# Ring, split units and attention tail of a hybrid mixer with 32 experts: five expert steps into dead buffers, high parts first, earlier splits

## The chip, the cores and the metric

One core of a Trainium2 chip runs one program. The time is the device time of a launch in microseconds, the median of three runs of the kernel before. TensorE, VectorE, ScalarE, GpSimd and SyncE each work through their own list of instructions and wait for each other by semaphores; SyncE does nothing but issue DMAs here.

## What is computed

Input `x` is 1 x 256 x 1024 in fp32. The first block adds to it a hybrid mixer and a mixture of experts, the second block four mixers: attention with a forgetting gate (`fox0`), gated linear attention (`gla`), gated delta net (`gdn`), and a second attention (`fox1`). Every layer begins with an RMS norm and two kinds of dense products, an input projection and an output projection. Cut to what matters here:

```python
def first_block(x, ...):
    hn = rmsnorm(h, norm_mix)                 # SSD + short convolution
    h = h + hybrid_mixer(hn, w_in, ..., w_out)
    hn = rmsnorm(h, norm_ffn)                 # 4 groups x 8 experts, best 2 of a group
    h = h + hierarchical_moe(hn, w_router_group, w_router_expert, w_gate, w_up, w_down)
    return rmsnorm(h, final_norm)
...
    def run_block(args):                      # one expert, d = 1024, f = 512
        return (jax.nn.silu(xb @ w_gate[e]) * (xb @ w_up[e])) @ w_down[e]
...
def fox_mixer(xn, w_in, b_f, q_gain, k_gain, w_out):
    q, k, v, z, f_logit = jnp.split(xn @ w_in, ...)      # 8 heads of 128
    ... p = softmax(q k / sqrt(dh) + (cum_q - cum_k), causal); o = p v
    return (o * jax.nn.silu(z)) @ w_out
```

## The kernel before

**Weights in a ring.** All big weights pass through `ring`, four slots of 2 MB (128 x 4096 fp32). SyncE loads a slot in two halves of 1 MB (`put`, lines 411 to 416) as soon as the slot's last user has released it (`released`, 326 to 332): a block of a dense layer is released when VectorE has split its last unit (`low_ready`), a step of the experts when TensorE has multiplied with it (`ring_used`). SyncE issues in program order: `ssd` (11 blocks of the input projection, 4 of the output projection), the experts, then `fox0`, `gla`, `gdn`, `fox1`.

**Dense units.** An fp32 product is made of three products of reduced operands (`F32R`): w_h x_h, w_h x_l and w_l x_h, with `_h` the rounded value and `_l` what is left. A block of weights has four units. For each unit ScalarE writes `w_h` (`high`, line 549), VectorE subtracts to get `w_l` (`low`, 919), each into one of three buffers (`PARTS`), so unit u waits until TensorE is done with u - 3. The activations lie as `hnT_h` and `hnT_l`; they are written by the norm (`norm_copies` 584, `norm` 967 and 971) and, ahead of an output projection, pair by pair of 128-row tiles by ScalarE (`out_high`, 573) and VectorE (`out_low`, 933). TensorE waits for `low_ready` of the unit and then runs it through `products` (lines 1669 to 1671), k after k, the three products of one k behind each other: in a `channels` unit 8 k x 3 matmuls of 256 columns with the weights stationary, in a `tokens` unit, and in all output projections, 2 token tiles x 2 k x 3 matmuls of 512 columns with the activations stationary. Who calls it: `project` (input), `gate_unit` (the eight gate units of an attention, one per head), `out_projection` (eight units, two k each; the first four wait for a pair of activations each). There are 132 units of the first kind and 72 of the second.

**Experts.** Eight quads of four experts, each quad 12 steps of 2 MB: 8 up steps (gate and up alternate; line 1892), 4 down steps (1913). Every expert has 32 places, so four experts fill the 128 columns of the array side by side. Between the up steps and the down steps of a quad stand the next quad's gather (1881), tanh on ScalarE (703), two products on VectorE, transposes; after the down steps the scatter (1924) and the sum into `x_res`. The first four steps are in the ring before the router is done; the other 92 are loaded when a slot comes free. The weights of all quads are read once (`passes` is 1 unless an expert has more than 32 tokens).

**Order around the experts.** The SSD layer ends with two groups of output units (`out_projection("ssd", [0])` and `[1]`; between them squares, their sums at 1721 and the spread at 1740), then transposes (1855), the router products (1862, which count `rt_done`), ranking on VectorE, gather, quad 0.

**Attention** (`fox`, three functions of the same name on ScalarE, VectorE, TensorE). After six projection blocks TensorE waits for all 12 bank copies, does gate unit 0, half of the key norms' spread (1740), gate unit 1, the other half, the scores of heads 0 and 1, and then per head h: gate unit h + 2, values of head h - 1 (2010 to 2012), transposes of the probabilities (2001), scores of head h + 2 (1992). ScalarE makes exponentials (743), copies the turned probabilities (749) and takes the gate's tanh (753); VectorE makes logits and their maxima (1365 to 1372), normalizes (1377 to 1379), gates (1385, 1393). In the same loops ScalarE and VectorE split the coming unit's weights (`high(z0 + h + 5)`, `low(z0 + h + 5)`), and from h = 6 on an output pair each. At the end TensorE runs

```python
                values(5)
                turn(6)
                out_projection(name, steps=[0])
                values(6)
                turn(7)
                out_projection(name, steps=[1])
                values(7)
                out_projection(name, steps=range(2, 2 * UNITS))
```

Names of semaphores that the change uses: `sq_summed` (sums of squares done), `unit_done` (dense units done), `rt_done` (router products), `fox_l` (logits of a head), `hnT_high` and `hnT_own` (high halves of the norm's output by ScalarE and by VectorE), `hnT_split` (its low parts), `proj_copied` (bank copies).

## Time and profile before

| | |
|---|---|
| median of 3 runs | 1540.92 us (1537.5 to 1541.04) |
| profiled execution | 1547.07 us, span 1545.4 us |
| mean granted TensorE clock | 0.867 of full |
| TensorE busy | 1242.7 us (80%), 8062 matmuls |
| VectorE busy | 677.2 us (44%) |
| ScalarE busy | 424.3 us (27%) |
| read from HBM | 310.4 MB, 202 GB/s over the span |
| chain that ended last | TensorE 49%, DMA 25%, VectorE 8% |

The chain is the work that ended last, followed back from the end: half of it is TensorE's, a quarter are loads of expert weights. Busy shares are means over stages with different limits. Durations in the rows are of one profiled execution, whose own time stands 6.15 us above the median.

### The profile page before, as it was taken

The page shows a single profiled execution, that of the slowest core. Times are in us where ns is not written, and L with a number is a line of the kernel's source. Part 1 is how long each engine was busy: PE and PEld are TensorE (multiplying, and loading weights), DVE is VectorE, ACT ScalarE, POOL GpSimd, SP SyncE. Part 2 cuts the span into 40 slices and gives each one's busy share as a digit, 9 for nine tenths or more (in the row PEclk, how much of TensorE's full clock was granted, in tenths as well). Part 3 has the DMA queues.
Part 4 walks back from the last instruction along what each step waited for, and adds up shares of the span by engine and source line. Part 5 has one row for each costly group of instructions (what it writes and reads, how often), then busy time and mean ns, then how long its engine had stood idle before and what let it go on. Part 6 is the DMA issues. An engine that isn't in the chain of part 4 may idle for free.

```text
span 1545.4 us, 19645 instructions
## 1 busy us (share of the span) xinstructions
PE 1242.7 (80%) x8062; PEld 935.6 (61%) x8062; DVE 677.2 (44%) x1258; ACT 424.3 (27%) x619; POOL 6.1 (0%) x28
## 2 busy tenths in 40 slices
PE   4999778666766766667659997998899698889997
PEld 4999667421221221212239895787779698769896
DVE  4775664301101111011064475564478856454474
ACT  3544333100000000000035344452345222145343
POOL 1000000000000000000000000000000000000000
PEclk9999798787877777777779999897889899889999
DMA  8464113399999999999977533341325200046500
GB/s 292 121 222 171 55 55 114 134 410 409 410 409 410 409 410 409 410 409 410 409 228 174 154 110 110 109 164 55 109 95 166 68 1 1 1 109 168 160 1 28
DMA packets 119635, 312.52 MB, mean 202 GB/s; under 512 B 17051, under 2 KB 17274, under 8 KB 119562
## 3 DMA queue, kind: packets, MB, share of 16 engines
q1 hardware_dynamic: 116864, 310.78, 55.6%
q10 hardware_dynamic: 2698, 0.71, 0.2%
q8 instruction: 53, 0.87, 0.2%
q14 instruction: 20, 0.16, 0.0%
HBM read 310.42 MB, written 1.05 MB: 202 GB/s over the span
## 4 chain that ended last, share of the span: by engine, by line
PE 49%; DMA 25%; DVE 8%; issue 3%; ACT 2%; SPq 1%; DVEq 0%; ACTq 0%
DMA ring<-in_w_up 16%; PE bank L1669 10%; PE bank L1670 10%; PE bank L1671 10%; DMA ring<-in_w_down 9%; PE bank L1892 4%; PE bank L1721 2%; PE bank L1913 2%; PE bank L1662 2%; PE bank L2172 2%; PE bank L2165 1%; PE bank L1740 1%; PE bank L2164 1%; DVE w_l L919 1%; PE bank L1968 1%
## 5 line engine op out<-in xcount | busy, mean ns | idle before, releaser
L919 DVE TENSOR_TENSOR w_l<-ring,w_h 128x1024 fp32r<-128x1024 f32 x204 | 247.8, 1223 | 194.8 <-ACT w_h L549 193.3
L1669 PE MATMUL bank<-hnT_h,w_h 128*128 128x256 f32 x1056 | 304.7, 289 | 11.1 <-DVE w_l L919 5.8
L1670 PE MATMUL bank<-hnT_l,w_h 128*128 128x256 f32 x1056 | 300.7, 285 | 0.0
L1671 PE MATMUL bank<-hnT_h,w_l 128*128 128x256 f32 x1056 | 300.7, 285 | 0.0
L549 ACT ACTIVATE w_h<-ring 128x1024 fp32r<-128x1024 f32 x204 | 215.4, 1058 | 287.4 <-PE bank L1671 287.0
L1892 PE MATMUL bank<-ring,cm 128*32 128x512 f32 x1024 | 172.3, 810 | 105.2 <-DMA ring<-in_w_gate 52.1
L1669 PEld LDWEIGHTS bank<-hnT_h,w_h 128*128 128x128 f32 x1056 | 204.5, 194 | 17.3 <-issue 6.4
L1670 PEld LDWEIGHTS bank<-hnT_l,w_h 128*128 128x128 f32 x1056 | 204.7, 194 | 0.2
L1671 PEld LDWEIGHTS bank<-hnT_h,w_l 128*128 128x128 f32 x1056 | 204.6, 194 | 0.0
L1892 PEld LDWEIGHTS bank<-ring,cm 128*32 128x32 f32 x1024 | 32.5, 130 | 237.4 <-DMA ring<-in_w_up 86.6
L1669 PE MATMUL bank<-w_h,hnT_h 128*128 128x512 f32 x288 | 119.1, 414 | 14.0 <-DVE hnT_l L933 13.4
L1913 PE MATMUL bank<-ring,cm 128*32 128x512 f32 x512 | 78.1, 749 | 48.4 <-DMA ring<-in_w_down 42.9
L1670 PE MATMUL bank<-w_l,hnT_h 128*128 128x512 f32 x288 | 116.3, 404 | 0.0
L1671 PE MATMUL bank<-w_h,hnT_l 128*128 128x512 f32 x288 | 115.7, 402 | 0.0
L1273 DVE SCALAR_TENSOR_TENSOR cm<-cm,bank 128x512 f32<-128x512 f32 x8 | 5.5, 688 | 213.0 <-ACT cm L703 213.0
L703 ACT ACTIVATE cm<-bank 128x512 f32<-128x512 f32 x8 | 4.8, 597 | 279.7 <-PE bank L1892 279.7
L1913 PEld LDWEIGHTS bank<-ring,cm 128*32 128x32 f32 x512 | 15.9, 124 | 98.6 <-DMA ring<-in_w_down 64.2
L1669 PEld LDWEIGHTS bank<-w_h,hnT_h 128*128 128x128 f32 x288 | 57.0, 198 | 28.2 <-DVE hnT_l L933 14.9
L1671 PEld LDWEIGHTS bank<-w_h,hnT_l 128*128 128x128 f32 x288 | 56.7, 197 | 12.5
L1670 PEld LDWEIGHTS bank<-w_l,hnT_h 128*128 128x128 f32 x288 | 56.8, 197 | 11.8
L1283 DVE COPY cm<-bank 128x512 f32<-128x512 f32 x8 | 5.5, 692 | 121.5 <-PE bank L1913 121.5
L1881 PEld LDWEIGHTS bank<-cm,hn 128*128 128x128 f32 x288 | 39.0, 218 | 14.7 <-issue 12.5
(373 smaller groups left out, 1455.3 us busy)
## 6 DMA issues: line engine op xcount, KB each, us to landing
ring<-in_w_gate SPq DMA_DIRECT2D x64, 1024.0 KB, 14.0
ring<-in_w_up SPq DMA_DIRECT2D x64, 1024.0 KB, 15.8
ring<-in_w_down SPq DMA_DIRECT2D x64, 1024.0 KB, 16.1
ring<-in_fox_w_in SPq DMA_DIRECT2D x32, 1024.0 KB, 9.4
ring<-in_w_in SPq DMA_DIRECT2D x22, 1024.0 KB, 8.4
ring<-in_gla_w_in SPq DMA_DIRECT2D x12, 1024.0 KB, 6.4
ring<-in_gdn_w_in SPq DMA_DIRECT2D x12, 1024.0 KB, 6.2
ring<-in_w_out SPq DMA_DIRECT2D x8, 1024.0 KB, 6.3
```

The lines of the kernel that those rows point to most:

```text
L549: af(part(w_h, u, width), w, ACT.Copy).then_inc(s["high_ready"], 1)
L919: v.tensor_tensor(part(w_l, u, width), w, part(w_h, u, width).bitcast(F32), ALU.subtract).then_inc(s["low_ready"], 1)
L1662: x = mm(dst, w[:, k, :], hnT[:, k, :], start=(k == 0), stop=(k == KD - 1))
L1669: mm(dst, sh, mh, start=start, stop=False)
L1670: mm(dst, sh, ml, start=False, stop=False)
L1671: return mm(dst, sl, mh, start=False, stop=stop)
L1721: x = mm(bank[SUM_BANK][:, t * R:(t + 1) * R], sq[:, g % 2, i % 4, t * P:(t + 1) * P], pick(i), start=(i == 0 and t == 0), stop=(i == n - ...
L1740: x = mm(b2(6 + g % 2)[m * i:m * i + m, j, t * P:(t + 1) * P], heads[:, 1, a:a + 1].to_broadcast([P, m]), ident[:], start=True, stop=True)
L1881: x = mm(b4(5 + k // 4)[:, k % 4, :], hn[:, t, own], m_S[:, t, :], start=(t == 0), stop=(t == NT - 1))
L1892: x = mm(bank[a][CAP * e:CAP * (e + 1), :], m_xg[:, 2 * b + r, CAP * e:CAP * (e + 1)], w[:, e, r, :], start=(b == 0 and r == 0), stop=(b = ...
L1913: x = mm(bank[3 + n][CAP * e:CAP * (e + 1), :], m_ht[:, c * P + CAP * e:c * P + CAP * (e + 1)], w[:, e, n * BLK:(n + 1) * BLK], start=(c = ...
L2172: x = mm(b4(g_banks[hf][2])[:, h, :], QT[:, h, :], R[:, h, :], start=True, stop=True)
```

## The change

Three things. (1) Steps 4 to 8 of quad 0 (`EXTRA = 5`) don't go through the ring but into buffers that are dead between the SSD layer's end and `fox0`: `vtm` with `sq`, a part of `cm`, and the storage of the split buffers `hnT_h`, `hnT_l`, `w_h`, `w_l` (now laid under a tensor `spare`) with `hnT`. Each has its own semaphore, and SyncE issues them after step 3 behind waits for the buffers' last readers. Quad 0 is written out on TensorE ahead of the loop, which begins at quad 1; SyncE writes out quads 0 and 1. (2) `products` is gone: a unit does all its w_h x_h products, then all w_h x_l, then all w_l x_h, and waits for `low_ready` only ahead of the third group, for the activations' low parts ahead of the second. (3) In the attention, gate unit 0 waits for 9 bank copies, gate unit 1 for 12; output pairs 0 and 1 are split one head earlier, the splits of the weights of output units 2 and 3 go behind the loop, and output unit 0 waits for the logits of all heads, whose banks it writes.

```diff
+EXTRA = 5
...
-        _n += NQ * MOE_STEPS
+        _n += NQ * MOE_STEPS - EXTRA
...
-        hnT_h, hnT_l = sb("hnT_h", [P, KD, T], F32R), sb("hnT_l", [P, KD, T], F32R)
-        w_h, w_l = sb("w_h", [P, PARTS, UNIT], F32R), sb("w_l", [P, PARTS, UNIT], F32R)
+        with ExitStack() as parts:
+            def split(name, shape):
+                return parts.enter_context(nc.sbuf_tensor(name, shape, F32R))
+
+            hnT_h, hnT_l = split("hnT_h", [P, KD, T]), split("hnT_l", [P, KD, T])
+            w_h, w_l = split("w_h", [P, PARTS, UNIT]), split("w_l", [P, PARTS, UNIT])
+
+        spare = sb("spare", [P, 2 * KD * T + 2 * PARTS * UNIT])
...
-            return s["ring_used"], n - RING_BASE["moe"] + 1
+            e = n - RING_BASE["moe"]
+            return s["ring_used"], e + 1 + (EXTRA if e >= SLOTS else 0)
...
+        extra = [[vtm[:].rearrange("p a b -> p (a b)"), sq[:].rearrange("p a b c -> p (a b c)")],
+                 [cm_free[:, 0:H], cm_free[:, H:2 * H]], [spare[:, 0:H], spare[:, H:2 * H]],
+                 [spare[:, 2 * H:3 * H], spare[:, 3 * H:4 * H]], [spare[:, 4 * H:5 * H], hnTf]]
...
+                    n = RING_BASE["moe"]
+                    for q in (0, 1):
                         for j in range(MOE_STEPS):
-                            i = (base + j) % SLOTS
+                            k = j - SLOTS
+                            if q == 0 and 0 <= k < EXTRA:
+                                if k == 0:
+                                    sp.wait_ge(s["sq_summed"], 4)
+                                if k == 2:
+                                    sp.wait_ge(s["unit_done"], UNIT_BASE["ssd_out"] + 4 * UNITS)
+                                if k == EXTRA - 1:
+                                    sp.wait_ge(s["rt_done"], 1)
+                                for dst, src in moe_loads(extra[k], q, j):
+                                    sp.dma_start(dst, src).then_inc(extra_ready[k], 16)
+                            else:
+                                put(n, moe_loads(ring_halves(n % SLOTS), q, j))
+                                n += 1
+                    with sp.Fori(2, NQ) as q:
...
...
-                    high(z0 + h + 5)
+                    if h < FOX_H - 2:
+                        high(z0 + h + 5)
...
-                    if h >= 6:
-                        pair_high(h - 6)
+                    if h >= 5:
+                        pair_high(h - 5)
                 turned_copy(7)
-                pair_high(2)
+                high(z0 + FOX_H + 4)
                 pair_high(3)
...
...
-                    low(z0 + h + 5)
+                    if h < FOX_H - 2:
+                        low(z0 + h + 5)
                     if h >= 2:
                         gated(h - 2)
-                    if h >= 6:
-                        out_low(name, h - 6, tiles(4 + 2 * h, 2))
+                    if h == 5:
+                        out_low(name, 0, tiles(16, 2))
+                    if h == 6:
+                        out_low(name, 1, tiles(18, 2))
+                out_low(name, 2, tiles(20, 2))
+                low(z0 + FOX_H + 4)
                 gated(6)
-                out_low(name, 2, tiles(20, 2))
                 gated(7)
...
+            def channel_unit(dst, u, split=None):
+
+                wh, wl = part(w_h, u, P), part(w_l, u, P)
+                if split is not None:
+                    pe.wait_ge(s["hnT_high"], 2 * split + 2)
+                    pe.wait_ge(s["hnT_own"], 2 * split + 2)
+                pe.wait_ge(s["high_ready"], u + 1)
+                for k in range(KD):
+                    mm(dst, wh[:, k, :], hnT_h[:, k, :], start=(k == 0), stop=False)
+                if split is not None:
+                    pe.wait_ge(s["hnT_split"], 2 * split + 2)
+                for k in range(KD):
+                    mm(dst, wh[:, k, :], hnT_l[:, k, :], start=False, stop=False)
+                pe.wait_ge(s["low_ready"], u + 1)
+                for k in range(KD):
+                    x = mm(dst, wl[:, k, :], hnT_h[:, k, :], start=False, stop=(k == KD - 1))
+                x.then_inc(s["unit_done"], 1)
+
+            def token_unit(banks, u, m, first, last, pair=None):
+
+                wh, wl = part(w_h, u, BLK), part(w_l, u, BLK)
+                spots = [(banks[t], 2 * m + j, slice(t * P, (t + 1) * P), j) for t in range(NT) for j in (0, 1)]
+                if pair is not None:
+                    pe.wait_ge(s["out_high"], pair)
+                pe.wait_ge(s["high_ready"], u + 1)
+                for dst, k, tt, j in spots:
+                    mm(dst, hnT_h[:, k, tt], wh[:, j, :], start=(first and k == 0), stop=False)
+                if pair is not None:
+                    pe.wait_ge(s["out_low"], pair)
+                for dst, k, tt, j in spots:
+                    mm(dst, hnT_l[:, k, tt], wh[:, j, :], start=False, stop=False)
+                pe.wait_ge(s["low_ready"], u + 1)
+                for dst, k, tt, j in spots:
+                    x = mm(dst, hnT_h[:, k, tt], wl[:, j, :], start=False, stop=(last and k == KD - 1))
+                x.then_inc(s["unit_done"], 1)
...
+            def first_slot(q, j):
+                if SLOTS <= j < SLOTS + EXTRA:
+                    pe.wait_ge(extra_ready[j - SLOTS], 32)
+                    return extra[j - SLOTS]
+                n = RING_BASE["moe"] + (j if j < SLOTS else j - EXTRA)
+                pe.wait_ge(ready[n % SLOTS], slot_value(n))
+                return ring_halves(n % SLOTS)
...
-            with pe.Fori(0, NQ) as q:
+            pe_quad(0, 0, 0, first_slot, s["ring_used"])
+            with pe.Fori(1, NQ) as q:
...
...
-                pe.wait_ge(s["proj_copied"], PROJ_BASE[name] + 12)
+                pe.wait_ge(s["proj_copied"], PROJ_BASE[name] + 9)
                 gate_unit(name, occ, 0)
                 pe.wait_ge(s["fox_fall"], 4 * occ + 4)
                 keys([0, 1])
+                pe.wait_ge(s["proj_copied"], PROJ_BASE[name] + 12)
                 gate_unit(name, occ, 1)
...
                 turn(6)
+                pe.wait_ge(s["fox_l"], (occ + 1) * FOX_H)
                 out_projection(name, steps=[0])
```

## Rows read from the trace of the kernel before

**Rows 1.** The page's 40 slices: granted clock (tenths), bandwidth.
```profile
PEclk9999798787877777777779999897889899889999
...
GB/s 292 121 222 171 55 55 114 134 410 409 410 409 410 409 410 409 410 409 410 409 228 174 154 110 110 109 164 55 109 95 166 68 1 1 1 109 168 160 1 28
```

**Rows 2.** Timeline of SyncE's queue, 200 to 420: start, length, instruction.
```profile
268.48 0.88 SPq L415 DMA_DIRECT2D ring<-in_w_up  x2
300.68 0.88 SPq L415 DMA_DIRECT2D ring<-in_w_gate  x2
```

**Rows 3.** Line 415, 150 to 420: issue to landing.
```profile
DMA to landing us min/median/max: 5.0/9.8/18.8
```

**Rows 4.** Chain that ended last, 150 to 420: the router's products.
```profile
276.88 6.21 PE bank L1862 x32
```

**Rows 5.** Timeline, 296 to 372: TensorE in quad 0; idle before and its releaser.
```profile
298.69 7.07 PE L1892 MATMUL bank<-ring,cm 128*32 128x512 f32 x64 [1.47 <-DVE cm L1256]
...
308.61 3.54 PE L1892 MATMUL bank<-ring,cm 128*32 128x512 f32 x16 [2.84 <-DMA ring<-in_w_gate]
...
313.73 1.92 PE L1892 MATMUL bank<-ring,cm 128*32 128x512 f32 x16 [1.58 <-DMA ring<-in_w_up]
...
325.82 4.04 PE L1881 MATMUL bank<-cm,hn 128*128 128x128 f32 x32
...
331.20 1.92 PE L1913 MATMUL bank<-ring,cm 128*32 128x512 f32 x16 [0.69 <-ACT cm L707]
```

**Rows 6.** Timeline of TensorE, 770 to 790: the last expert step.
```profile
775.78 3.35 PE L1913 MATMUL bank<-ring,cm 128*32 128x512 f32 x16 [3.21 <-DMA ring<-in_w_down]
```

**Rows 7.** Costliest groups: busy, mean ns | idle before, releaser.
```profile
L1669 PE MATMUL bank<-hnT_h,w_h 128*128 128x256 f32 x1056 | 304.7, 289 | 11.1 <-DVE w_l L919 5.8
...
L1669 PE MATMUL bank<-w_h,hnT_h 128*128 128x512 f32 x288 | 119.1, 414 | 14.0 <-DVE hnT_l L933 13.4
```

**Rows 8.** Timeline, 18 to 25.6: before the first unit.
```profile
21.96 2.93 ACT L549 ACTIVATE w_h<-ring 128x1024 fp32r<-128x1024 f32 x3
...
25.29 0.55 PE L1669 MATMUL bank<-hnT_h,w_h 128*128 128x256 f32 x1 [3.92 <-DVE w_l L919]
```

**Rows 9.** Timeline, 240 to 249: second output group of SSD.
```profile
246.55 0.63 ACT L573 ACTIVATE hnT_h<-cm 128x512 fp32r<-128x512 f32 x1 [8.05 <-DVE cm L1181]
...
247.96 0.79 PE L1669 MATMUL bank<-w_h,hnT_h 128*128 128x512 f32 x1 [2.44 <-DVE hnT_l L933]
```

**Rows 10.** Timeline, 885 to 893: first gate unit of an attention.
```profile
887.60 0.39 PE L1669 MATMUL bank<-hnT_h,w_h 128*128 128x256 f32 x1 [2.18 <-ACT vtm L592]
...
888.78 0.41 PE L1669 MATMUL bank<-hnT_h,w_h 128*128 128x256 f32 x1
...
891.97 1.27 PE L1740 MATMUL bank<-ident,heads 128*128 128x128 f32 x9
```

**Rows 11.** Timeline, 926 to 945: tail of an attention.
```profile
929.66 0.49 PE L2001 MATMUL bank<-ident,cm 128*128 128x128 f32 x3
...
929.98 0.41 DVE L1372 TENSOR_REDUCE cm<-cm 128x1 f32<-128x256 f32 x1
...
932.84 0.55 PE L1669 MATMUL bank<-w_h,hnT_h 128*128 128x512 f32 x1 [2.69 <-DVE hnT_l L933]
...
937.29 0.38 PE L2010 MATMUL bank<-cm,vtm 128*128 128x128 f32 x2
...
940.86 0.50 PE L1669 MATMUL bank<-w_h,hnT_h 128*128 128x512 f32 x1 [2.40 <-DVE hnT_l L933]
...
943.69 0.38 PE L2010 MATMUL bank<-cm,vtm 128*128 128x128 f32 x2
...
944.28 0.48 PE L1669 MATMUL bank<-w_h,hnT_h 128*128 128x512 f32 x1
```

**Rows 12.** Timeline of VectorE, 128 to 141: low parts, one a unit.
```profile
135.38 1.23 DVE L919 TENSOR_TENSOR w_l<-ring,w_h 128x1024 fp32r<-128x1024 f32 x1 [1.65 <-ACT w_h L549]
138.26 1.23 DVE L919 TENSOR_TENSOR w_l<-ring,w_h 128x1024 fp32r<-128x1024 f32 x1 [1.65 <-ACT w_h L549]
```

More of the change, by code:

```diff
@@ L254, in build @@
         ready = [sem(f"slot_ready{i}") for i in range(SLOTS)]
+        extra_ready = [sem(f"extra_ready{i}") for i in range(EXTRA)]
         ov_ready, ov_used = sem("ov_ready"), sem("ov_used")
@@ L1673, in gate_unit @@
             def gate_unit(name, occ, h):
-                u = UNIT_BASE[name] + UNITS * FOX_Z + h
                 if h >= 2:
                     pe.wait_ge(s["fox_z"], occ * FOX_H + h - 1)
-                pe.wait_ge(s["low_ready"], u + 1)
-                wh, wl = part(w_h, u, P), part(w_l, u, P)
-                for k in range(KD):
-                    x = products(bank[2 + h % 2][:, 0:T], (wh[:, k, :], wl[:, k, :]),
-                                 (hnT_h[:, k, :], hnT_l[:, k, :]), k == 0, k == KD - 1)
@@ L1683, in gate_unit @@
-                x.then_inc(s["unit_done"], 1)
+                channel_unit(bank[2 + h % 2][:, 0:T], UNIT_BASE[name] + UNITS * FOX_Z + h)
             def project(name, first, end):
@@ L1753, in out_projection @@
                             u = UNIT_BASE[name + "_out"] + UNITS * (2 * g + n) + m
[L1754 to L1764 removed]
+                            token_unit([bank[t + 2 * n][:] for t in range(NT)], u, m, g == 0, g == OUT_GROUPS[name] - 1,
+                                       PAIR_BASE[name] + 4 * g + m + 1 if n == 0 else None)
             pe.wait_ge(s["ident_ready"], 1)
```

77 lines of the change are left out of this document (25 added, 52 removed).

## The prediction

> **What bounds the kernel now.** I read the page's 40 slices first. From slice 9 on, for twelve slices, the core moves 409 to 410 GB/s, and before them come four slices with 55 to 134 GB/s [rows 1]: the experts are bound by their weights, and the stage before them leaves the DMA engines nearly idle. Next SyncE's queue. The fourth and last weight step that the ring can hold is issued at 268.48, the fifth only at 300.68, when TensorE has used up the first [rows 2]. A step is 2.1 MB. The quickest landing of a 1 MB half is 5.0 us [rows 3]; 2.56 of it is transfer (below), so some 2.4 is latency, and the last step of the ring has landed at 268.5 + 2.4 + 5.1 = 276.0. Then nothing moves for 27 us. TensorE's rows show what the experts do: four steps run in one go from 298.69 in 7.07 us, 1.77 each, then each waits for DMA; steps 4 and 5 start 5.12 apart (308.61, 313.73) [rows 5]. The last starts at 775.78 [rows 6], so 91 steps took 467.17, 5.13 each: no transfer stalls in between. So in the experts only fewer steps, or an earlier start of the transfers, help.
>
> The rest of the time is TensorE's. In the dense parts it works without gaps but for waits that the groups of instructions name: 5.8 us in all for low parts of weights, 13.4 for low parts of activations [rows 7]. Single gaps are in the timelines: 3.92 at the start [rows 8], 2.44 before the second output group of SSD [rows 9], 2.18 before the first gate unit of an attention layer [rows 10], 2.69 and 2.40 before its first two output units [rows 11]. A gap costs more than itself: after the 2.18 the matmuls of 256 columns fall from 0.12 us to 0.213 at 888.78 (15 of them fill 888.78 to 891.97 [rows 10]), which is the 1.2 GHz level of the two, and they ran at 2.4 before the gap.
>
> **The change, part by part.** *Five expert steps ahead.* Their DMAs are no more than before, ten of 1 MB; they are issued after the fourth step's at 268.48. Steps 4 and 5 wait for the fourth sum of squares, passed by then; 6 and 7 for the last output unit of SSD, which the router stage from 273 on follows; step 8 for the router's products, done at 276.88 + 6.21 = 283.1 [rows 4]. SyncE has nothing else queued behind these waits than the ring's later loads, which can't start before 300.68 anyway. At 5.12 a step they land at 281, 286, 291, 296 and 301.6; the last is used after 318, see below. In a sentence of its own: the Trainium skill (DMA: Bandwidth & Descriptors, "Where 436 GB/s comes from") has the HBM side bind HBM-to-SBUF transfers at about 358 GB/s; by it a step would take 5.86 and five 29.3, but the slices' 410 speaks against it, and the measurement decides.
>
> Gain at most 5 x 5.12 = 25.6. What can eat it: nine steps are there, but only four ring slots. Their loads are issued from 300.68 on as steps 0 to 3 are used: steps 9 to 12 land at 308.2, 313.4, 318.5, 323.6. Steps 4 to 8 free no slot. TensorE does steps 0 to 7 at 1.77 from 298.69: 312.8. From the end of the last up step to the first down step is gather, tanh and transposes: 325.82 to 331.20, 5.38 [rows 5], so step 8 starts at 318.2 and step 9 is released at 318.2 + 2 x 1.92 = 322.0. Its slot's next load moves from 324.7 on: DMA idle for 1.1. Step 13 lands at 329.8; before, 308.6 + 9 x 5.13 = 354.8. **Gain 25.0.** From quad 1 on all is as before, 82 more steps at 5.13. Bounds: 25.6 if nothing stalls; 7.6 if TensorE does all of quad 0 at 3.54 a step, as step 4 [rows 5]. I take the first kind, since the four steps from 298.69 ran at 1.77 behind continuous work, and the new ones follow them without a gap.
>
> *High parts first.* Each dense unit (24 matmuls of 256 columns or 12 of 512) now waits for the high part of its weights, and for the low part two thirds later. Number and shape of the matmuls stay. At the start the first high part is ready at 21.96 + 0.98 = 22.94 (2.93 for three) instead of 25.29 [rows 8]: 2.3. The rest of the 5.8 is 1.9 in two equal gaps, where VectorE was busy and the high part waiting: 1.7, with the 0.2 for what remains. Output units: 0.6 for low weights (14.0 less 13.4 [rows 7]). SSD's second group starts when the high part of pair 0 is there, 246.55 + 0.63 = 247.2 instead of 247.96 [rows 9]: 0.8, and GLA's first pair, which has the same pattern, 0.7. Sum 6.1. The low parts hide behind two thirds of a unit (1.9 us against 1.23 for one); were VectorE later than that, the wait would come back in mid-unit, never longer than before. The SSD part reaches the end since the 27 us from 268.48 move as a whole. Bounds: 0 (gap moved to mid-unit) and 8.
>
> The added waits: one more in each of 204 units and some 24 for pairs. No row shows a wait between matmuls of one unit. The nearest: VectorE's low parts, one a unit, start at 135.38 and 138.26, 2.88 apart [rows 12], and 2.88 is 24 x 0.12, so the wait at a unit's head costs nothing. From above: a whole matmul, 0.29 [rows 7]. I take 0; the head's wait is nearest in kind.
>
> *Attention, first gate unit.* It waits for 9 bank copies, not 12, and those are long done. TensorE goes on at 887.60 - 2.18 = 885.42 and at the full clock, done at 885.42 + 2.88 = 888.3 instead of 891.97 [rows 10]: 3.7. Low parts were ready (TensorE waited for ScalarE's copies alone); VectorE was idle and takes the spread products earlier. Two layers: **7.3**. Bounds: 2.2 and 3.7 each.
>
> *Attention, output pairs.* Old: TensorE is free at 929.66 + 0.49 = 930.15, output unit 0 starts at 932.84 and, slow after the gap, ends at 937.29; values and turn take until 938.46 (940.86 - 2.40); unit 1 runs from 940.86 to 943.69 (2.83, full clock), values, then unit 2 at 944.28 [rows 11]. New: pair 0 is split a head earlier, as soon as the last gate unit has read the buffers. Its low part (some 0.7, like the high part's 0.63 [rows 9]) stands on VectorE ahead of head 6's probabilities and pushes the logits of head 7, which ended at 929.98 + 0.41 = 930.39, to about 930.8; the new wait on them is what now ends last. Unit 0 runs 930.8 to 933.7, values and turn (1.17) to 934.9, unit 1 to 937.7, values 0.59, unit 2 at 938.3 instead of 944.28: 6.0. Late next: weights of unit 2 and 3, whose splits are put behind the last turned copy, then pair 3. By this count the turned copy ends about 935.6 and the high part of unit 2 at 936.6; VectorE's two low parts (2.46), two gatings (0.8, two operations of 128x256 like the 0.41 above) and ScalarE's 0.63 make pair 3 ready at 940.6; TensorE wants it at 938.3 + 2.8 = 941.1. That cover is thin: without it 1 to 2 us a layer. Two layers: **12.0**. Bounds: 2.5 and 7 each.
>
> **Sum:** 25.0 + 6.1 + 7.3 + 12.0 = 50.4. The profiled execution took 1547.1 (span 1545.4 and 1.7 around it), so 1496.7; it stood 6.2 above the median of the runs, and against that median, 1540.9, the forecast is 1490.5.
>
> **The rivals.** *Cold first quad:* TensorE runs quad 0 at 3.54 a step. For it: step 4 did in the old trace [rows 5], and the mean clock there is 0.7 to 0.8 [rows 1]. Against: those stood behind idle time, which is gone. The slots come free at 339.5, step 13 lands at 347.2, the experts give 7.6: 1508. *Late code:* the first quad of TensorE is now written out ahead of the loop, while transfers fill the DMA engines from 268 on. If a block of code had to queue behind weights, the first step would start late by up to the longest landing in that stretch, 18.8 [rows 3], and all of it would count: 1509. Against: in the experts' stage before, with full DMA, no wait of that kind shows. In a sentence of its own: the Trainium skill (Runtime: NRT & Kernel Launch, "Instruction fetch mechanics") says code is prefetched in sequence and a taken branch outside the window stalls; no row here shows such a stall. *Tail turned, not gained:* splits of units 2 and 3 or pair 3 come late and VectorE's order keeps the old end; of the 12.0 some 5 stay: 1497.5. *Slower:* the waits between matmuls of one unit stop the overlap of neighbours, in all 204 units. Price a whole matmul, 0.29, for 228 waits: 66 us, 15.7 more than the gain: 1556.6. It decides from 50.4 / 228 = 0.22 a wait. Against it stand rows 12. *The change does nothing:* the early loads were hidden anyway; excluded by the 27 us without transfers.
>
> **How the numbers follow.** Forecast 0.70, cold quad 0.12, late code 0.04, tail 0.10, slower 0.03; nothing 0.01. The range, 1482 to 1510, takes in the bounds of the small terms (8 better by clock and pairs) and the first three rivals; what is left out is the slower case and sizes off by more. About 0.3% (4.6 us) is what a measurement of this kernel can tell from no change. Faster is all but the last two: 0.95 with a little taken off for mixtures, same 0.02, slower 0.03.
>
> **What would show it.** Right: weights move without a pause from 268 minus about 5, nine steps run before the first DMA wait; the 1 MB issues of step 9 begin right after the first step; no gap before the first gate unit; output unit 0 waits below 1 us and takes 2.83; the idle for low parts at lines of the dense products falls from 19 to below 5. Wrong: steps of quad 0 at 3.5; a wait for the slots after it; units longer than 2.88 and 2.83; output units 2 or 3 waiting.

## The result and the profile after

| | before | after |
|---|---|---|
| median of 4 runs each, us | 1539.21 | 1488.49 |
| lowest to highest | 1533.98 to 1541.04 | 1486.63 to 1493.44 |
| profiled execution: its time / its span | 1547.1 / 1545.4 | 1486.6 / 1484.9 |
| mean granted clock in it | 0.867 | 0.913 |

The changed kernel takes 0.9681 of the time (95% interval 0.9646 to 0.9716), 49.1 us less, between 43.7 and 54.5. The forecast was 50.4 less, at 1490.5. The two spans are 60.5 apart, more than the medians: the profiled execution of before took 6 us more than the slowest of its runs shown, and that of after is the fastest of its own. A later comparison of the same two kernels on another occasion (e9_again below) gave 0.9651.

The page of the changed kernel, its slices of clock and bandwidth and the dense products. Line 1713 is the first third of a unit of 256 columns, line 1731 of a unit of 512; columns as in [rows 7].

```profile
span 1484.9 us, 19587 instructions
PE 1197.7 (81%) x8062; PEld 917.4 (62%) x8062; DVE 677.0 (46%) x1258; ACT 424.3 (29%) x619; POOL 6.1 (0%) x28
...
PEclk9999798898998988989879998996899899889999
...
GB/s 284 103 255 196 57 57 114 386 409 409 410 409 410 410 410 410 410 409 410 407 204 177 159 114 114 115 218 8 113 114 170 58 1 1 1 114 167 118 58 29
...
L1713 PE MATMUL bank<-hnT_h,w_h 128*128 128x256 f32 x1056 | 151.5, 286 | 3.1 <-ACT w_h L587 2.2
...
L1731 PE MATMUL bank<-w_h,hnT_h 128*128 128x512 f32 x288 | 81.5, 406 | 3.0 <-ACT hnT_h L611 1.7
```

As many matmuls as before. The slice that moved 134 GB/s in [rows 1] moves 386 now. Waits for low parts, 5.8 and 13.4 us in [rows 7], are gone from the list; of what is left in these groups, 3.1 and 3.0, the page puts 2.2 and 1.7 down to high parts.

SyncE's queue, start and length; to set beside [rows 2]:

```profile
260.00 0.88 SPq L440 DMA_DIRECT2D ring<-in_w_up  x2
260.92 0.47 SPq L468 DMA_DIRECT2D vtm<-in_w_gate  x1
...
262.18 1.20 SPq L468 DMA_DIRECT2D cm<-in_w_up  x2
...
276.58 2.31 SPq L468 DMA_DIRECT2D hnT<-in_w_down  x1
290.47 4.78 SPq L440 DMA_DIRECT2D ring<-in_w_down  x6
295.62 4.58 SPq L440 DMA_DIRECT2D ring<-in_w_gate  x2
311.43 0.88 SPq L440 DMA_DIRECT2D ring<-in_w_up  x2
```

The ten early loads are issued from 260.92 on, the last at 276.58, and windows of 4 us from 262.4 to 278.4 carry 387, 416, 372 and 418 GB/s, so the stream doesn't stop. The ring is filled again from 290.47 on, when the first slot is free. TensorE in quad 0, to set beside [rows 5]; the last entry in brackets is the idle time before and what ended it:

```profile
288.48 7.07 PE L1935 MATMUL bank<-ring,cm 128*32 128x512 f32 x64 [1.38 <-DVE cm L1295]
...
298.81 3.62 PE L1935 MATMUL bank<-spare,cm 128*32 128x512 f32 x32
302.35 4.04 PE L1924 MATMUL bank<-cm,hn 128*128 128x128 f32 x32
...
309.47 5.33 PE L1956 MATMUL bank<-ring,cm 128*32 128x512 f32 x48
315.82 3.67 PE L1967 MATMUL bank<-cm 128*128 128x512 f32 x8 [1.02 <-DVE cm L1322]
...
321.52 1.92 PE L1935 MATMUL bank<-ring,cm 128*32 128x512 f32 x16 [0.18 <-DMA ring<-in_w_up]
326.64 3.62 PE L1935 MATMUL bank<-ring,cm 128*32 128x512 f32 x16 [3.20 <-DMA ring<-in_w_gate]
```

Two steps of `spare` take 3.6 us, three of the ring 5.3: all run at 1.8 a step. The first wait for a transfer is 0.18 long and stands at step 13, the second of quad 1. From step 14 on the old pace of one step per 5.1 us is back.

**Where the time went.** The trace was cut at the first matmul of each stage. The table gives the length of the stages that the change touches most, for all fourteen profiles: up to the first dense unit; from it to the transposes behind SSD's projection (SSD 1); SSD's state and first output group up to the spread of its second (SSD 2); the experts, from their first matmul to the last quad's scatter; and for each attention the stage up to its first scores (the first gate unit lies in it) and from there to the next norm or the end (the tail lies in it).

| kernel | start | SSD 1 | SSD 2 | experts | gate 1 | tail 1 | gate 2 | tail 2 |
|---|---|---|---|---|---|---|---|---|
| before | 25.3 | 136.6 | 63.0 | 481.4 | 103.8 | 66.3 | 105.3 | 65.1 |
| after | 22.2 | 134.5 | 60.9 | 455.9 | 100.5 | 60.0 | 101.5 | 58.7 |
| e1_noextra | 22.9 | 135.3 | 61.7 | 480.9 | 100.5 | 60.0 | 101.5 | 58.8 |
| e2_extraonly | 24.9 | 136.7 | 62.8 | 456.7 | 106.0 | 66.3 | 105.4 | 65.1 |
| e3_lateextra | 22.4 | 135.4 | 61.6 | 463.0 | 102.0 | 60.0 | 101.4 | 58.8 |
| e4_extra3 | 22.8 | 134.5 | 60.9 | 466.8 | 102.0 | 59.9 | 101.4 | 58.8 |
| e5_unitsold | 25.0 | 136.6 | 62.9 | 457.5 | 99.8 | 60.0 | 101.4 | 58.8 |
| e6_gate12 | 22.6 | 134.5 | 61.0 | 458.3 | 105.9 | 59.9 | 105.5 | 58.8 |
| e7_tailold | 22.9 | 134.6 | 60.9 | 454.4 | 99.8 | 62.9 | 101.4 | 63.1 |
| e8_waits | 22.2 | 134.7 | 61.7 | 455.9 | 100.5 | 59.9 | 101.5 | 58.7 |
| e9_again | 22.2 | 134.7 | 61.1 | 457.3 | 99.8 | 60.0 | 101.4 | 58.7 |
| e10_tail2 | 22.1 | 134.9 | 60.9 | 457.5 | 100.4 | 59.6 | 101.5 | 58.4 |
| e11_slowquad | 22.9 | 135.4 | 61.7 | 462.8 | 102.0 | 60.0 | 101.4 | 58.7 |
| e12_soonextra | 22.8 | 134.5 | 61.7 | 455.9 | 100.4 | 60.0 | 101.5 | 58.7 |

From before to after the eight columns give 25.5 + 3.1 + 2.1 + 2.1 + 7.1 + 12.7 = 52.6. Of the 3.1 at the start 0.9 is not the change's: the input had landed earlier, since the norm's transposes started at 15.94 and not at 16.86. To it comes 0.7 outside the columns, SSD's second output group, which waits 1.71 instead of 2.44 [rows 9]. That makes 52.4. The other 8 us of the 60.5 are the 0.9 of the start, 0.5 in the rest of SSD's second output group, 1.7 between it and the experts, 3.1 in GLA and 1.8 in GDN. In GLA's dense units two waits for low parts are gone, 0.73 and 0.24 us long. The rest is not told apart from what one kernel does by itself: in the profiles of kernels that have the same code in these stages as the changed one, the stage between SSD and the experts takes 23.4 to 25.1, GLA 146.2 to 153.4 and GDN 251.2 to 254.9.

Three columns need such a measure too. With the same code, SSD 1 takes 134.5 to 135.4 and SSD 2 60.9 to 61.7, and gate 1 takes 99.8 to 102.0; gate 2 and the tails repeat within 0.2. And the column of the experts holds the last step, which TensorE ran at different clocks. Windows from its start to the scatter (start and end, length; busy time of PE, PEld, DVE, ACT, POOL; clock; DMA share; GB/s), first before:

```profile
775.78:780.12 4.34, 3.35 (x16) 0.62 (x17) 0.69 (x1) 0.60 (x1) 0.00 (x0) 0.61 1.05 386
```

then after:

```profile
741.42:744.36 2.94, 1.92 (x17) 0.45 (x17) 0.69 (x1) 0.60 (x1) 0.00 (x0) 1.00 1.05 385
```

So 1.4 of the 25.5 is the clock of the last step. From the first expert matmul to the start of the last step it took 477.08 before and 452.94 after, 24.1 less.

### The profile page after: what moved, and what is told of

It reads as the page before. It is cut to its first block, busy times and chain, and to the rows that moved or that the text cites. A ratio compares the mean times of both kernels' runs of the same rounds, so it can differ in the third digit from the quotient of the medians.

```text
span 1484.9 us, 19587 instructions
## 1 busy us (share of the span) xinstructions
PE 1197.7 (81%) x8062; PEld 917.4 (62%) x8062; DVE 677.0 (46%) x1258; ACT 424.3 (29%) x619; POOL 6.1 (0%) x28
## 4 chain that ended last, share of the span: by engine, by line
PE 50%; DMA 25%; DVE 8%; issue 3%; ACT 1%; SPq 1%; DVEq 0%; ACTq 0%
DMA ring<-in_w_up 17%; DMA ring<-in_w_down 8%; PE bank L1713 6%; PE bank L1720 6%; PE bank L1717 6%; PE bank L1731 5%; PE bank L1735 5%; PE bank L1738 4%; PE bank L1935 3%; PE bank L1774 2%; PE bank L1701 2%; PE bank L2221 2%; PE bank L2214 2%; PE bank L1793 2%; PE bank L1956 1%
## 5 line engine op out<-in xcount | busy, mean ns | idle before, releaser
L1935 PE MATMUL bank<-ring,cm 128*32 128x512 f32 x960 | 149.9, 756 | 111.3 <-DMA ring<-in_w_gate 67.2
L1713 PE MATMUL bank<-hnT_h,w_h 128*128 128x256 f32 x1056 | 151.5, 286 | 3.1 <-ACT w_h L587 2.2
L1717 PE MATMUL bank<-hnT_l,w_h 128*128 128x256 f32 x1056 | 149.0, 284 | 0.0
L1720 PE MATMUL bank<-hnT_h,w_l 128*128 128x256 f32 x1056 | 148.7, 284 | 0.0
L1713 PEld LDWEIGHTS bank<-hnT_h,w_h 128*128 128x128 f32 x1056 | 136.7, 192 | 8.1 <-issue 4.5
L1717 PEld LDWEIGHTS bank<-hnT_l,w_h 128*128 128x128 f32 x1056 | 137.0, 193 | 0.0
L1720 PEld LDWEIGHTS bank<-hnT_h,w_l 128*128 128x128 f32 x1056 | 136.8, 193 | 0.0
L1956 PE MATMUL bank<-ring,cm 128*32 128x512 f32 x496 | 70.9, 700 | 45.5 <-DMA ring<-in_w_down 40.7
L1731 PE MATMUL bank<-w_h,hnT_h 128*128 128x512 f32 x288 | 81.5, 406 | 3.0 <-ACT hnT_h L611 1.7
L1735 PE MATMUL bank<-w_h,hnT_l 128*128 128x512 f32 x288 | 78.7, 396 | 0.0
L1738 PE MATMUL bank<-w_l,hnT_h 128*128 128x512 f32 x288 | 77.9, 393 | 0.0
```

What stands on the lines that cost most here:

```text
L1713: mm(dst, wh[:, k, :], hnT_h[:, k, :], start=(k == 0), stop=False)
L1717: mm(dst, wh[:, k, :], hnT_l[:, k, :], start=False, stop=False)
L1720: x = mm(dst, wl[:, k, :], hnT_h[:, k, :], start=False, stop=(k == KD - 1))
L1731: mm(dst, hnT_h[:, k, tt], wh[:, j, :], start=(first and k == 0), stop=False)
L1735: mm(dst, hnT_l[:, k, tt], wh[:, j, :], start=False, stop=False)
L1738: x = mm(dst, hnT_h[:, k, tt], wl[:, j, :], start=False, stop=(last and k == KD - 1))
```

## The experiments

They ran in three sets, up to e4, up to e8 and up to e12, and the kernel before, run beside each, had medians of 1541.61, 1542.59 and 1542.89. All edits but that of e2_extraonly are made in the changed kernel. Profiles carry the verdict where the effect is small: each interval is about 0.35% to each side, some 5 us.

**e1_noextra: all but the early steps.** `-EXTRA = 5` `+EXTRA = 0` (the list of buffers is shortened to as many).

> The changed kernel with EXTRA = 0: all expert steps go through the ring again, the rest of the change stays. Theory (the experts are bound by their transfers, and each step loaded ahead is worth its 5.12 us): the stage from the first expert matmul to the last scatter is 481.4 us again, the DMA engines idle for about 25 us before it, and of the gain some 25.5 us go: about 1514 us, ratio to the kernel before 0.984. Rival (the dense parts brought most, the experts' gain is partly a side effect of a warmer TensorE): more than 1520 us is not reached, and the stage stays below 475.

1512.11 us, ratio 0.9802 [0.977, 0.9835]. The experts take 480.9 again, as before (477.2 to the start of the last step); every other column is within 0.8 of the changed kernel's.

**e2_extraonly: the early steps alone.** The kernel before with the new loads, `spare` and the written-out first quad; units, gate wait and tails are the old ones; only the new wait for all heads' logits stays in.

> The kernel before with the five early steps alone (units, gate wait and tail as before). Theory: only the experts' stage gets shorter, by 25.6 us, all other stages keep their lengths within what the clock does by itself: 1513.5 us, ratio 0.9834. With the run without early steps this tells whether the parts add up. Rival (parts depend on each other): the sum of both gains differs from 50.7 us by more than 8.

1519.58 us, 0.9837 [0.9796, 0.9877]. Experts 456.7, all else within 0.4 of before but for gate 1, which is 2.2 longer, as much as it differs between executions of the changed kernel. The median stands 6 above the 1513.5 that was expected, and the stages don't say why. The two halves give 30.5 and 25.1 by their ratios, 55.6 in all, against 49.1 and 53.8 for the whole: they add up within their intervals. The early steps are worth 24.7 here and 25.0 beside e1_noextra; up to the start of the last step, 24.3 in both.

**e3_lateextra: the same loads, started later.**

```diff
                                     sp.wait_ge(s["sq_summed"], 4)
+                                    sp.wait_ge(s["rt_done"], 1)
```

> The changed kernel, but the five early steps are issued only after the router's products (some 12 us later), still long before they are used. Theory (what counts is that the transfers run without a pause from step 3 on): the DMA engines idle for about 7 us between step 3 and step 4, the experts end 7 us later relative to the router, about 1495.5 us. Rival (what counts is only that nine steps are there when the experts begin, the number of buffers): no change, 1488.5 us; steps 4 to 8 are on time in both.

1495.77 us, 0.969 [0.9654, 0.9727]. The experts take 463.0, 7.1 more. The DMA share and bandwidth in windows of 4 us (length; busy time of PE, PEld, DVE, ACT, POOL; clock; DMA share; GB/s) show the pause:

```profile
266.00:270.00 4.00, 1.97 (x16) 1.73 (x16) 2.95 (x7) 2.91 (x8) 0.00 (x0) 1.00 0.97 384
270.00:274.00 4.00, 3.78 (x32) 3.67 (x32) 3.19 (x15) 0.00 (x0) 0.00 (x0) 0.96 0.07 28
274.00:278.00 4.00, 0.00 (x0) 0.00 (x0) 3.55 (x19) 1.06 (x6) 0.00 (x0) 0.50 0.70 217
278.00:282.00 4.00, 2.34 (x10) 2.21 (x10) 2.54 (x15) 0.00 (x0) 0.00 (x0) 0.50 1.03 416
```

Against a steady 410, the windows of 28, 217 and 384 GB/s lost 3.7, 1.9 and 0.3 us of transfer, 5.9 in all. From the first expert matmul to the start of the last step the kernel took 458.7, 5.8 more than the changed one; the other 1.3 of the 7.1 is the last step, at the lower clock again. The loads must not only be early, the stream must not pause.

**e4_extra3: three early steps.** `-EXTRA = 5` `+EXTRA = 3` (the list of buffers is shortened to as many).

> The changed kernel with three early steps instead of five. Theory (5.12 us a step): 10.2 us slower, 1498.7 us. Rival (the first steps bring more than the last, since the ring's own refill hides some): less than 6 us slower.

1498.79 us, 0.9714 [0.9682, 0.9747]; experts 466.8, 10.9 more for two steps less. Of it 1.3 is the last step at the lower clock; up to its start the stage is 9.6 longer, 4.8 for each step against the 5.12 of a transfer.

**e5_unitsold: the old order of products and one wait at the unit's head.**

```diff
-                pe.wait_ge(s["high_ready"], u + 1)
-                for k in range(KD):
-                    mm(dst, wh[:, k, :], hnT_h[:, k, :], start=(k == 0), stop=False)
...
                 pe.wait_ge(s["low_ready"], u + 1)
                 for k in range(KD):
+                    mm(dst, wh[:, k, :], hnT_h[:, k, :], start=(k == 0), stop=False)
+                    mm(dst, wh[:, k, :], hnT_l[:, k, :], start=False, stop=False)
                     x = mm(dst, wl[:, k, :], hnT_h[:, k, :], start=False, stop=(k == KD - 1))
```

(not shown: the waits for the activations' parts, and the same edit in the units of 512 columns)

> The changed kernel with the units as before: one wait for the low part at the head, the three products of one k behind each other. Theory: the 19 us of waits for low parts come back as far as the new tail doesn't hide them, that is 2.3 at the start, 1.7 in two gaps of SSD, 0.8 each before the second output group of SSD and the first pair of GLA, plus what the clock loses after them: 6 to 9 us slower, 1495 to 1497 us. Rival (the order of the products itself costs or saves, since neighbours share the stationary operand no more): the pace within units changes from 0.12 us a matmul, and the time moves by more than 12 us or not at all.

1489.79 us (1486.76 to 1499.11), 0.9655 [0.9619, 0.9691]: in the time this can't be told from the changed kernel, a miss. In the stages it can: 25.0, 136.6 and 62.9, as before the change, 2.8, 2.1 and 2.0 more than after (0.6 of the first is again the input's landing), so 6.3. Against all profiles with the new units, whose SSD 1 and SSD 2 vary by 0.9 and 0.8, it is 4.6 to 6.3. TensorE's timeline shows the old gap:

```profile
24.97 0.55 PE L1712 MATMUL bank<-hnT_h,w_h 128*128 128x256 f32 x1 [3.92 <-DVE w_l L958]
```

**e6_gate12: the old wait of the gate unit.**

```diff
-                pe.wait_ge(s["proj_copied"], PROJ_BASE[name] + 9)
+                pe.wait_ge(s["proj_copied"], PROJ_BASE[name] + 12)
                 gate_unit(name, occ, 0)
```

> The changed kernel, but gate unit 0 of both attention layers waits for all 12 bank copies again. Theory: a gap of 2.18 us before it and a unit at half clock after it, 3.7 us a layer, 7.3 us in all: 1495.8 us. Rival (the gap is worth itself alone, the clock comes back by itself elsewhere): 4.4 us, 1492.9 us.

1497.11 us (1487.19 to 1507.17), 0.9692 [0.9647, 0.9737]. The gap is back, and after it the half clock (8 matmuls in 1.91 us at 863.29 where the changed kernel needs 1.12):

```profile
860.82 1.22 PE L1713 MATMUL bank<-hnT_h,w_h 128*128 128x256 f32 x8 [2.18 <-ACT vtm L630]
...
863.29 1.91 PE L1720 MATMUL bank<-hnT_h,w_l 128*128 128x256 f32 x8
```

The stages take 105.9 and 105.5 against 99.8 to 102.0 and 101.4 to 101.5: 3.9 to 6.1 in the first, 4.0 to 4.1 in the second. The rival of 2.2 each, the gap alone, falls.

**e7_tailold: the old order of the tail's splits.**

```diff
-                    if h >= 5:
-                        pair_high(h - 5)
+                    if h >= 6:
+                        pair_high(h - 6)
...
-                    if h == 5:
-                        out_low(name, 0, tiles(16, 2))
-                    if h == 6:
-                        out_low(name, 1, tiles(18, 2))
-                out_low(name, 2, tiles(20, 2))
-                low(z0 + FOX_H + 4)
+                    if h >= 6:
+                        out_low(name, h - 6, tiles(4 + 2 * h, 2))
                 gated(6)
+                out_low(name, 2, tiles(20, 2))
```

(not shown: the splits of the weights of output units 2 and 3 go back into the loop, the high part of pair 2 behind it)

> The changed kernel with the attention's splits in the order of before (pair 0 at head 6, weights of output units 2 and 3 in the loop). Theory: the gaps before output units 0 and 1 come back, less the 0.7 that the early high part saves each: 1 to 1.5 us a gap and the slow unit after it, in all 4 to 5 a layer, 8 to 10 us: 1497.5 us. Rival (with high parts first alone the gaps are short enough for the clock to hold): 3 to 4 us in all, 1492 us.

1495.94 us, 0.9692 [0.9658, 0.9726]. The tails take 62.9 and 63.1, so 2.9 + 4.4 = 7.3 of the 12.7 go. TensorE's timeline in the first tail, with output units 0 and 1:

```profile
895.39 1.16 PE L1726 MATMUL bank<-w_h,hnT_h 128*128 128x512 f32 x4 [1.88 <-issue]
...
900.09 1.20 PE L1726 MATMUL bank<-w_h,hnT_h 128*128 128x512 f32 x4 [0.73 <-ACT hnT_h L611]
901.76 1.20 PE L1730 MATMUL bank<-w_h,hnT_l 128*128 128x512 f32 x4 [0.47 <-DVE hnT_l L971]
```

Both units wait again: for unit 0 the profile names no releaser (its high part was being made from 894.68 on, for 0.61), unit 1 waits for its high part and once more in its middle for the low one. With e5_unitsold and e2_extraonly this makes a table of two by two for both tails: neither edit 66.3 and 65.1, high parts first alone 62.9 and 63.1, the new order alone 60.0 and 58.8, both 60.0 and 58.7. So the order alone gives the whole gain; where it stands, high parts first add nothing in the tails, and without it they would give 5.4.

**e8_waits: fourteen more waits in each unit of 256 columns,** 1848 in all, each for a value that the semaphore has long had.

```diff
                 for k in range(KD):
+                    if k:
+                        pe.wait_ge(s["high_ready"], u + 1)
                     mm(dst, wh[:, k, :], hnT_h[:, k, :], start=(k == 0), stop=False)
```

(and the same with `low_ready` in the last third)

> The changed kernel with 14 more waits in each of the 132 units of 24 matmuls, one ahead of each matmul of the first and third group but the first, all on semaphores that have their value already: 1848 waits. Theory (a wait that is met costs TensorE nothing while its matmuls take 0.12 us): no change, 1488.5 us, units still 2.88 us. Rival (a wait stops the overlap of neighbouring matmuls, 0.17 us or more each): over 300 us slower. In between, 0.01 us a wait would show as 18 us.

1487.85 us (1483.05 to 1488.93), 0.9632 [0.9597, 0.9667]. VectorE's low parts, one a unit, start as far apart as in [rows 12]:

```profile
127.42 1.23 DVE L958 TENSOR_TENSOR w_l<-ring,w_h 128x1024 fp32r<-128x1024 f32 x1 [1.58 <-ACT w_h L587]
130.30 1.23 DVE L958 TENSOR_TENSOR w_l<-ring,w_h 128x1024 fp32r<-128x1024 f32 x1 [1.65 <-ACT w_h L587]
```

130.30 - 127.42 = 2.88. A wait that is met costs nothing that can be measured here, between matmuls of one sum too.

**e9_again: the changed kernel, unedited,** to see how much two profiles of one kernel differ.

> The changed kernel once more, unedited, as the measure for the runs beside it: 1487 to 1490 us, ratio 0.965 to 0.968. Theory (what differs between executions of the same code is TensorE's clock): some stages of this profile are 1 to 3 us longer or shorter than in the first profile of it, with the same busy time of VectorE and ScalarE; the stage of the experts is 455.9 us within 1, since transfers set it. Rival: stages repeat within 0.3 us.

1487.63 us (6 runs, 1486.38 to 1489.24), 0.9651 [0.9622, 0.9681], 53.8 us less than before. The experts' stage came out at 457.3, 1.4 more and so not within the 1 that was expected. Up to the start of the last step it took 452.7, against 452.9 in the first profile; the difference is the last step, which ran at a clock of 0.50. GLA differs by more than the 3 expected: 146.2 against 152.9. The windows of both stages are in the last section.

**e10_tail2: pair 0's low part a little later in VectorE's order,** behind the logits of head 7 that TensorE waits for.

```diff
                         logits(h + 1)
+                        if h == 6:
+                            out_low(name, 0, tiles(16, 2))
...
-                    if h == 5:
-                        out_low(name, 0, tiles(16, 2))
```

> The changed kernel with the low part of pair 0 put on VectorE behind the logits of head 7 instead of ahead of head 6's probabilities. Theory (the logits of head 7 are what output unit 0 waits for, 0.63 us, and the low part is needed only two thirds of a unit later): the gap before output unit 0 goes below 0.3 us, 0.4 us a layer, 0.8 us in all, which the times can't show and the profile can. Rival (the low part is late then and the wait moves into the unit): unit 0 gets longer by as much.

1486.35 us (1483.45 to 1492.07), 0.9643 [0.9611, 0.9676]. Output unit 0 waits 0.30 instead of 0.63, and the tails take 59.6 and 58.4, 0.7 less in all: seen in the profile, not to be told in the time.

**e11_slowquad: the gather of quad 0 done three times,** so that the first down step comes later.

```diff
-                gather(g + 1, it + 1)
+                gather(g + 1, it + 1, times=3 if wait_slot is first_slot else 1)
```

> The changed kernel with the gather's matmuls of quad 0 done three times (the same result again), 8.1 us more work on TensorE between step 7 and step 8. Theory (five of nine early steps free no ring slot, so a slower quad 0 leaves the DMA engines idle): the DMA engines pause for 7 to 8 us before step 13, and the stage of the experts grows by as much, from 455.9 to 463.5 us. Rival (four slots and the order of landing hide more than I counted): growth below 4 us.

1494.98 us, 0.9697 [0.9658, 0.9736]. TensorE does 11.57 instead of 4.04, 7.5 more, and the experts take 462.8, 6.9 more. The windows behind it, columns as above:

```profile
312.60:316.60 4.00, 4.00 (x36) 3.91 (x35) 0.47 (x1) 0.25 (x1) 0.00 (x0) 1.00 1.03 410
316.60:320.60 4.00, 3.31 (x34) 1.07 (x36) 0.82 (x2) 0.73 (x2) 0.00 (x0) 1.00 0.14 56
320.60:324.60 4.00, 3.91 (x40) 0.91 (x28) 0.02 (x1) 0.02 (x1) 0.00 (x0) 1.00 0.60 181
324.60:328.60 4.00, 3.08 (x7) 1.44 (x8) 0.67 (x1) 0.57 (x1) 0.00 (x0) 1.00 0.87 313
```

Against 410 the last three lost 3.5, 2.2 and 0.9, together 6.6 us of transfer, so 0.9 of the 7.5 was absorbed, or 0.6 by the stage's length. That is all the slack that the ring's release has in quad 0: TensorE must have freed a slot by the time the ninth step ahead has landed. Since the stream has no pause left in the changed kernel, a sixth early step would find no idle transfer time; it wasn't run.

**e12_soonextra: the loads of steps 4 and 5 issued ahead of those of steps 2 and 3,** to have more bytes under way during SSD.

```diff
+                            if q == 0 and j == 2:
+                                sp.wait_ge(s["sq_summed"], 4)
+                                for e in (0, 1):
+                                    for dst, src in moe_loads(extra[e], 0, SLOTS + e):
+                                        sp.dma_start(dst, src).then_inc(extra_ready[e], 16)
```

> The changed kernel with steps 4 and 5 issued ahead of steps 2 and 3, when the fourth sum of squares is there, into the pause of the DMA engines before step 2. Theory (nine buffers are all there is, and the changed kernel's transfers already run on into the ring's refill): the pause of 16 us shrinks, one of about 10 us appears behind step 8, and the stage of the experts stays at 455.9 us within 1. Rival (an earlier start of the stream is worth what it is earlier): 8 to 10 us faster.

1488.3 us (1482.57 to 1489.32), 0.9645 [0.9604, 0.9686]; experts 455.9, as in the changed kernel. Windows behind step 8:

```profile
283.50:287.50 4.00, 4.00 (x24) 4.00 (x23) 0.00 (x0) 0.00 (x0) 0.00 (x0) 0.59 0.51 205
287.50:291.50 4.00, 2.62 (x27) 1.19 (x29) 2.18 (x6) 0.00 (x0) 0.00 (x0) 1.00 0.02 4
291.50:295.50 4.00, 4.00 (x42) 1.17 (x36) 0.00 (x0) 0.00 (x0) 0.00 (x0) 1.00 0.68 224
```

The bytes come sooner, the stream then pauses until the first slot of the ring is free (7.8 us of transfer are lost against 410), and nothing is won that these profiles can tell. Up to the start of the last step it took 451.5 instead of 452.9, which is about the slack of e11_slowquad, but the other kernels with five early steps and an unbroken stream lie between 451.4 and 453.7 here. With the release of the ring on the other side, transfers that start sooner only wait sooner.

## Why the prediction was right

**Early steps:** forecast 25.0, measured 25.5 in the profile, 25.0 and 24.7 in the halves; without the clock of the last step it is 24.1, 24.3 and 24.3. Quad 0 at full clock (1.77; 1.8) came as said. The stream started 2 us sooner than said (268 less 5; the first early load was issued at 260.9), and thirteen steps, not nine, ran before the first wait for a transfer, since the refill kept up. What failed are the two pauses that the forecast put into the stream: 1.5 between the landing of step 8 at 301.6 and the refill's first bytes (300.68 and 2.4 of latency), which its sum holds without naming, and the stall of 1.1 before step 13. In windows of 4 us from 278 to 326 the changed kernel moves 406 to 412 GB/s, so neither is there. From the fourth step's issue to the first expert matmul 288.48 - 260.00 = 28.5 passed, not the 298.69 - 268.48 = 30.2 of before, and step 9 was released 311.43 - 288.48 = 22.95 after that matmul, not 23.3. The two give 2.05, which turns the missing 1.1 into 0.95 of slack, and e11_slowquad measured 0.6 to 0.9. The stage up to the experts is not touched by the change; its 1.7 is one execution against another (e5_unitsold and e7_tailold have it at its old length), and the slack goes with it. Where 30.1 passed, in e5_unitsold, the stream dips in two windows, 397 GB/s from 300 to 304 and 371 from 320 to 324: 0.1 and 0.4 us, not 1.5 and 1.1.

**High parts first:** forecast 6.1, of it 5.4 in the start and SSD (2.3, 1.7, 0.6 and 0.8); measured there 2.2 + 2.1 + 2.1 + 0.7 = 7.1, and the first three give 4.6 to 6.3 by e5_unitsold. The first and the last came as forecast; what was too small are the 1.7 and the 0.6. The row of the start:

```profile
22.22 1.47 PE L1713 MATMUL bank<-hnT_h,w_h 128*128 128x256 f32 x8 [2.17 <-ACT w_h L587]
```

The first unit stood at 25.29 before. Those two were sized from the idle times of the profile, and a gap costs more than its idle time even where the clock holds. TensorE's timeline of the kernel before at the first of SSD 1's two gaps:

```profile
108.74 0.28 PE L1671 MATMUL bank<-hnT_h,w_l 128*128 128x256 f32 x1
109.83 0.39 PE L1669 MATMUL bank<-hnT_h,w_h 128*128 128x256 f32 x1 [0.81 <-DVE w_l L919]
110.05 0.28 PE L1670 MATMUL bank<-hnT_l,w_h 128*128 128x256 f32 x1
```

A matmul is 0.28 long in the profile, but the next starts 0.12 after it. The idle time is counted from its end, so 0.81 of it are 1.09 from start to start, 0.97 more than the pace, and the next matmul follows after 0.22, another 0.10. Behind it they start 0.12 apart again, at the full clock. That makes 1.07 for each of the two gaps, which is SSD 1's 2.1. The third gap, 0.69 long before a unit of SSD's first output group, costs 0.94 in the same way (225.13 to 226.21, then 226.52, at a pace of 0.227); SSD 2 gains another 0.3 to 1.2 beyond it, in a stage that varies by 0.8 by itself, so whether more than the gap is in it stays open. The 0.7 for GLA's first pair is there: from the spread to the first output unit 4.51 passed before (1088.53 to 1093.04) and 3.78 after (1042.16 to 1045.94), though GLA's stage as a whole varies by too much to show it.

**Gate unit:** forecast 3.7 a layer, measured 3.3 and 3.8, and about 4 in the second layer by e6_gate12. In the changed kernel there is no gap before the unit, and a third of it takes 0.95:

```profile
849.25 1.07 PE L1738 MATMUL bank<-w_l,hnT_h 128*128 128x512 f32 x4
850.16 1.12 PE L1713 MATMUL bank<-hnT_h,w_h 128*128 128x256 f32 x8
851.11 1.12 PE L1717 MATMUL bank<-hnT_l,w_h 128*128 128x256 f32 x8
```

**Output pairs:** forecast 6.0 a layer, measured 6.3 and 6.4. TensorE's timeline in the first tail:

```profile
890.60 0.49 PE L2050 MATMUL bank<-ident,cm 128*128 128x128 f32 x3
891.72 1.20 PE L1731 MATMUL bank<-w_h,hnT_h 128*128 128x512 f32 x4 [0.63 <-DVE cm L1411]
...
895.49 1.17 PE L1731 MATMUL bank<-w_h,hnT_h 128*128 128x512 f32 x4
...
898.89 1.18 PE L1731 MATMUL bank<-w_h,hnT_h 128*128 128x512 f32 x4
...
901.75 1.07 PE L1731 MATMUL bank<-w_h,hnT_h 128*128 128x512 f32 x4
```

Counted from the moment when TensorE is free (891.09), unit 0 starts after 0.63, unit 1 after 4.4, unit 2 after 7.8; forecast were 0.65, 4.75 and 8.15, and before it was 14.13 for unit 2 [rows 11]. The new wait that I named, the logits of head 7, is the one that ends last, and e10_tail2 halves it by moving the split named as its cause. The cover for pair 3 that I called thin held: its unit starts at 901.75 with no wait.

**The rivals.** Cold first quad: excluded by 1.8 a step. Late code: no wait of that kind shows in quad 0, where TensorE runs through its twelve steps while 406 to 412 GB/s of transfers are under way. By the rule of the Trainium skill (Runtime: NRT & Kernel Launch, "Instruction fetch mechanics") straight code is prefetched, and the new code is straight; the trace doesn't contradict it. Slower by waits: excluded by e8_waits; 1848 of them left the units 2.88 apart and the median within 1 us of the other two of this kernel (its interval, 5 us to each side, allows 0.003 each), where 0.22 each was needed. Tail turned: excluded by the tails' columns. The stage of the experts moved 409 GB/s in the mean, so the bound of 358 that the Trainium skill (DMA: Bandwidth & Descriptors, "Where 436 GB/s comes from") gives is passed after the change as it was before, by a program on one core.

**The sum:** 25.0 + 6.1 + 7.3 + 12.0 = 50.4 forecast; 25.5 + 7.1 + 7.1 + 12.7 = 52.4 in the profiles. The medians give 49.1 and 53.8 with intervals of some 5 to each side, which hold both. The parts were right in kind and near in size, each shown by a run of its own; that the sum came within 2 us is in part luck, since 1.4 of the 25.5 is the last step's clock and SSD and gate 1 vary by 1 to 2 us between executions of one kernel.

## What to carry to other kernels

Where a stage is bound by transfers, and the engines ahead of it leave the queues idle, a step loaded ahead is worth one transfer time each, as long as the stream never pauses: count from the last free slot to the first release, for the pauses came back nearly one for one (5.9 lost, 5.8 longer; 6.6 lost, 6.9 longer). In an accumulated product begin with the operands that are ready and put the wait where the late operand is used; a met wait cost nothing that could be measured, while a gap costs more than its idle time: 1.07 us for 0.81 where the clock held, and about 4 for 2.18 where it fell behind the gap. Judge edits of a few us by the length of the stages in several profiles: the time of whole runs could not tell some 5 us that three stages showed plainly. Look at where a stage ends, too: here the clock of its last step moved the length by 1.4.

## What the runs showed of the hardware

**The mean clock of an execution doesn't give its time.** Two stages of the changed kernel in two executions, the experts and GLA (columns: start and end, length; busy time of PE, PEld, DVE, ACT, POOL; clock; DMA share; GB/s). First after:

```profile
288.48:744.36 455.88, 291.61 (x1897) 91.76 (x1897) 51.32 (x100) 17.39 (x32) 0.00 (x0) 0.90 1.03 409
920.61:1073.54 152.93, 137.25 (x793) 120.96 (x793) 82.09 (x130) 60.01 (x75) 0.00 (x0) 0.86 0.32 111
```

then e9_again:

```profile
291.21:748.53 457.32, 319.41 (x1897) 105.45 (x1897) 51.31 (x100) 17.39 (x32) 0.00 (x0) 0.77 1.03 409
926.32:1072.50 146.18, 130.44 (x792) 116.58 (x792) 81.97 (x130) 60.00 (x75) 0.00 (x0) 0.91 0.33 116
```

In the experts the clock is 0.90 once and 0.77 once, and the stage differs by 1.4 us of 456, all of it in the last step; up to there the transfers set the pace. In GLA it is 0.86 and 0.91, and the same code takes 152.9 and 146.2, though VectorE and ScalarE are busy for the same time. Over whole executions the clock was 0.913 and 0.875, with spans of 1484.9 and 1484.7. What puts an execution's fast and slow stretches where they are was not tried.

**A core can stream weights at 409 GB/s in the mean of 456 us.** The slices within the stage read 409 or 410; the last, in which the transfers end, reads 407.
